# A hybrid decoder step: the inverse's transpose kept in the chunk recurrence, and every second paged sample gathered turned

## What is computed

```python
# the chunk recurrence, for each head and chunk
a_mat = where(strict, beta * (k @ k.T) * decay, 0) + eye(chunk)
w_v = solve(a_mat, v * beta)            # unit lower triangular
w_k = solve(a_mat, k * beta * exp(G))
# the paged decode, for each of 8 samples: 32 pages of 128 positions
past_c = cache_latent[page_table]       # 4096 x 256
past_r = cache_krope[page_table]        # 4096 x 64
past_k = cache_kscale[page_table]       # 4096 x 8
s = (q_lat @ c.T + q_rope @ kr.T) * ksc * SOFTMAX_SCALE
o_lat = softmax(s) @ c
```

## Time and profile before

| | |
|---|---|
| median of 3 runs | 3991.21 us |
| the profiled execution | 3988.52 us, of which the span is 3986.4 |
| TensorE, weight load, VectorE, ScalarE, GpSimd busy | 75%, 36%, 62%, 39%, 32% of the span |
| mean granted TensorE clock | 0.849 of 2.4 GHz |
| the chunk recurrence | 303.7 to 636 us |
| `mla_qkv` and the paged decode | 2205 to 2234 and 2234.6 to 2465.3 us |

### The profile page before, as it was taken

The page is one execution under the profiler, slowest core; times in us unless marked ns, Lnnn a source line. Parts: engine busy times, 40 slices in busy tenths (PEclk is TensorE's granted clock), DMA queues, the critical chain, the costliest instruction groups (busy, mean ns, idle before and its releaser), DMA issues. The chain is left out here.

```text
span 3986.4 us, 45941 instructions
## 1 busy us (share of the span) xinstructions
PE 3005.8 (75%) x14557; PEld 1439.4 (36%) x14557; DVE 2474.6 (62%) x6084; ACT 1535.0 (39%) x4402; POOL 1289.7 (32%) x1172
## 2 busy tenths in 40 slices
PE   7997888777666677768757798776777876666666
PEld 6886775322212122223313575322232222222221
DVE  2665443676676667767773343476677677667675
ACT  2352121444343344446432221344544444334332
POOL 0004330444434333333441110233334344334433
PEclk9998788988778788888878898888888988787778
DMA  2211002999999999999996453799999999999998
GB/s 89 73 51 55 13 13 71 404 420 416 420 414 418 405 397 387 411 366 384 402 421 244 165 204 144 291 375 390 381 375 415 405 404 421 413 420 413 411 421 334
DMA packets 234350, 1261.33 MB, mean 316 GB/s; under 512 B 32008, under 2 KB 71952, under 8 KB 97552
## 3 DMA queue, kind: packets, MB, share of 16 engines
q0 software_dynamic: 153600, 1133.58, 69.8%
q1 hardware_dynamic: 80528, 125.08, 9.1%
HBM read 1244.25 MB, written 14.19 MB: 316 GB/s over the span
## 5 line engine op out<-in xcount | busy, mean ns | idle before, releaser
L1951 PE MATMUL acc<-ring,diag 128*64 128x512 f32 x4096 | 1339.0, 751 | 751.3 <-ACT diag L1650 748.9
L1569 POOL DMA_INDIRECT ring<-in_uv,idx x1024 | 1119.1, 1093 | 1895.3 <-PE acc L1951 1635.2
L1761 DVE SCALAR_TENSOR_TENSOR ring<-ring,rep 128x1024 f32<-128x1024 f32 x1024 | 1230.6, 1221 | 368.9 <-DMA ring<-in_uv,idx 309.3
L1951 PEld LDWEIGHTS acc<-ring,diag 128*64 128x64 f32 x4096 | 250.3, 158 | 1494.2 <-ACT diag L1650 1317.8
L1642 ACT ACTIVATE hg<-hs 128x1 f32<-128x1 f32 x1024 | 203.7, 199 | 1141.1 <-DVE ring L1761 1139.1
L1650 ACT ACTIVATE diag<-const,hgg 128x64 f32<-128x64 f32 x1024 | 356.4, 348 | 33.4
L1646 ACT ACTIVATE hgg<-hg,weigh_by 128x1 f32<-128x1 f32 x1024 | 302.0, 295 | 33.2
L1883 PE MATMUL big<-xnT,w 128*128 128x264 f32 (+1 forms) x960 | 297.1, 435 | 0.0
L1883 PEld LDWEIGHTS big<-xnT,w 128*128 128x128 f32 x960 | 174.8, 203 | 185.0 <-issue 166.4
L298 PE MATMUL acc<-xnT,w 128*128 128x260 f32 x1024 | 230.2, 386 | 0.7 <-ACT inp L419 0.7
L298 PEld LDWEIGHTS acc<-xnT,w 128*128 128x128 f32 x1024 | 196.3, 192 | 38.4 <-issue 7.5
(11 more groups left out here) (571 smaller groups left out, 4057.7 us busy)
## 6 DMA issues: line engine op xcount, KB each, us to landing
w<-in_w_peer SPq DMA_DIRECT2D x64, 512.0 KB
w<-in_w_gdn SPq DMA_DIRECT2D x32, 512.0 KB, 3.6
ring<-in_uv,idx POOLq DMA_INDIRECT x1024, 12.3
wo<-in_w_mla_out SPq DMA_DIRECT2D x8, 1024.0 KB, 11.5
wo<-in_w_uq SPq DMA_DIRECT2D x8, 768.0 KB, 14.2
out_ssm_s<-states SPq DMA_DIRECT2D x4, 1024.0 KB, 5.1
wo<-in_w_gdn_out SPq DMA_DIRECT2D x4, 1024.0 KB, 8.2
sk<-in_keys SPq DMA_DIRECT2D x64, 64.0 KB
```

The lines of the kernel that those rows point to most:

```text
L1569: pool.indirect_dma_start(out=ring[:, c % RING, :], out_offset=None, in_=uv, in_offset=bass.IndirectOffsetOnAxis(ap=idx[u % 2][:, c:c + 1] ...
L1761: dve.scalar_tensor_tensor(ring[:, c % RING, 0:D], ring[:, c % RING, 0:D], 1.0, rep[:, 2 * a + c // RING, :], ALU.mult, ALU.mult, accum_ou ...
L1951: last = pe.matmul(acc[i][rows(j), :], diag[:, r, :], ring[:, r, D + HALF * j:D + HALF * j + HALF], start=r == 0, stop=r == RING - 1)
```

## The change

Three edits, made together.

In `gdn_seq`, `U` is turned only once per pair, before level 0, and all of it is copied to `T`. In levels 0 to 4 a second product of `U` and `X` follows each step on TensorE, and VectorE adds it into `T`, as it adds the step into `U`. VectorE's order at the head of a pair is changed: both heads' `U` first, then `Kb`, `kd`, `Vb` and `qk`.

In `mla_dec`, samples with `a` = 1 get their scores from a second copy of the cache, `cache_turned`, which is laid out in advance with 128 rows per page: a row is a latent (or rotary) channel and holds 320 numbers, 1280 bytes. It is fetched page by page, 32 indirect gathers of 128 rows (`pages_turned`), into one tile `turned`. These samples have no transposes and no copies of them; their latents are fetched as before for the value product, their rotary keys aren't. GpSimd's loop is written out, and in it the turned pages stand before the odd sample's factors and latents.

In `mla_qkv`, row numbers for these gathers are made from the page table: two more small loads on SP and three more VectorE operations on 256 columns.

```diff
@@ gdn_seq, ScalarE
-                    for j in range(LV):
-                        for a in range(2):
-                            after(act, at("flipped", i, 2 * j + a + 1))
-                            act.activation(half(T[a], j, 0), half(pC[a], j, 0), ACT.Copy).then_inc(s["flip_out"], 1)
+                    for a in range(2):
+                        after(act, at("flipped", i, a + 1))
+                        act.activation(T[a][:, :, :], pC[a][:, :, :], ACT.Copy).then_inc(s["flip_out"], 1)
+                    for j in range(LV):
@@ gdn_seq, TensorE
+                    for a in range(2):
+                        after(pe, at("seeded", i, 2 * a + 2))
+                        turn(pC[a], U[a]).then_inc(s["flipped"], 1)
                     for j in range(LV):
                         for a in range(2):
-                            after(pe, at("seeded", i, 2 * a + 2) if j == 0 else at("grown", i, 2 * (j - 1) + a + 1))
-                            turn(pC[a], U[a]).then_inc(s["flipped"], 1)
-                        for a in range(2):
-                            after(pe, at("flip_out", i, 2 * j + a + 1), at("lmask", i, 2 * j + a + 1))
+                            after(pe, at("paired_up", i, 2 * (j - 1) + a + 1) if j else at("flip_out", i, a + 1), at("lmask", i, 2 * j + a + 1))
...
-                            some(pB[a], X[j % 2][a], U[a], j, 1).then_inc(s["stepped"], 1)
+                            if j:
+                                after(pe, at("grown", i, 2 * (j - 1) + a + 1))
+                            last = some(pB[a], X[j % 2][a], U[a], j, 1)
+                            if j < LV - 1:
+                                last = some(pC[a], U[a], X[j % 2][a], j, 0)
+                            last.then_inc(s["stepped"], 1)
@@ gdn_seq, VectorE
                         for a in range(2):
                             after(dve, at("stepped", i, 2 * j + a + 1))
+                            if j < LV - 1:
+                                dve.tensor_tensor(half(T[a], j, 0), packed(pC[a]).rearrange("p (b s) -> p b s", s=2 << j), half(T[a], j, 0), ALU.add).then_inc(s["paired_up"], 1)
                             dve.tensor_tensor(half(U[a], j, 1), packed(pB[a]).rearrange("p (b s) -> p b s", s=2 << j), half(U[a], j, 1), ALU.add).then_inc(s["grown"], 1)
@@ mla_qkv, VectorE
+                dve.tensor_copy(pages.rowf[:, :], pages.all[:, :]).then_inc(s["gains"], 1)
...
+                dve.scalar_tensor_tensor(pages.rowf[:, :], pages.rowf[:, :], float(PAGE), pages.lane[:, 0:1].to_broadcast([P, NS * PAGES]), ALU.mult, ALU.add).then_inc(s["gains"], 1)
+                dve.wait_ge(s["gains"], 3)
+                dve.tensor_copy(pages.row[:, :], pages.rowf[:, :])
@@ mla_dec, GpSimd
+                def pages_turned(v):
+                    for g in range(PAGES):
+                        pool.indirect_dma_start(out=turned[:, g, :], out_offset=None, in_=core.i["cache_turned"],
+                                                in_offset=bass.IndirectOffsetOnAxis(ap=pages.row[:, PAGES * v + g:PAGES * v + g + 1], axis=0)).then_inc(s["lt1"], 16)
...
+                keys()
+                latents(0)
+                factors(0)
+                pages_turned(1)
+                latents(1)
+                factors(1)
+                for i in range(1, TURNS):
+                    after(pool, at("idx", i - 1, 1), at("flip", i - 1, NG))
+                    keys()
+                    after(pool, at("soft0", i - 1, 1))
+                    factors(0)
+                    after(pool, at("pv", i - 1, 1))
+                    latents(0)
+                    after(pool, at("idx", i - 1, 2), at("dotted", i - 1, 2 * NG))
+                    pages_turned(2 * i + 1)
+                    after(pool, at("soft1", i - 1, 1))
+                    factors(1)
+                    after(pool, at("pv", i - 1, 2))
+                    latents(1)
@@ mla_dec, TensorE
+                def latent(a, g, e, j):
+                    if a == 0:
+                        return cT[g % 2][:, e, j, :]
+                    first = PAGE * e + GRP * (BQ * g + j)
+                    return turned[:, :, first:first + GRP]
...
+                        if a and g == 1:
+                            after(pe, at("lt1", i, 16 * PAGES))
+                        after(pe, at("lined", i, n - 1))
                         if g == 1:
                             after(pe, at("staged", i, 2 * a + 2))
                         scores(a if g else 1 - a, (g - 1) % NG)
...
+                    if a:
+                        after(pe, (s["lc1"], i * 16 + 16), (s["ld1"], i * 16 + 16))
@@ mla_dec, VectorE
-                                apart(dve, at(f"lc{a}", i, 16), at(f"ld{a}", i, 16), at(f"lr{a}", i, 16), at(f"lk{a}", i, 16))
+                                apart(dve, at(f"lc{a}", i, 16), at(f"ld{a}", i, 16), at(f"lk{a}", i, 16))
+                                if a == 0:
+                                    apart(dve, at("lr0", i, 16))
                                 number(2 * i + 2 + a, a)
```

More of the change, by code:

```diff
@@ L510, in gdn_seq @@
     with Marks(core, "seq", rowed=4, summed=2, diff=4, decay=4, masks=4, made=2, signed=2,
[L511 removed]
+               crossed=2, turned=2, products=4, scaled=6, seeded=4, flipped=2, flip_out=2, paired_up=2 * (LV - 1), lmask=2 * LV, joined=2 * LV,
                joined_out=2 * LV, stepped=2 * LV, grown=2 * LV, wk=2, wk_out=2, u_made=2 * NT, u_out=2 * NT, s_made=2 * NT,
@@ L574, in _ @@
                             if j == 0:
-                                after(pool, at("products", i, 2 * a + 1))
+                                after(pool, at("products", i, a + 1))
                             if j >= 2:
@@ L762, in _ @@
                         dve.tensor_tensor(U[a][:, :, :], U[a][:, :, :], mask(C_ID), ALU.add).then_inc(s["seeded"], 1)
+                    for a in range(2):
+                        h = 2 * i + a
                         after(dve, at("turned", i, a + 1))
@@ L2152, in _ @@
                 sp.dma_start(pages.rest[:, :], core.i["rest"]).then_inc(s["page"], 16)
+                sp.dma_start(pages.lane[:, :], core.i["lane"]).then_inc(s["page"], 16)
+                sp.dma_start(pages.all[:, :], core.i["page_table"].rearrange("(o b) g -> o (b g)", o=1).to_broadcast([P, NS * PAGES])).then_inc(s["page"], 16)
                 sp.dma_start(pages.wukT[:, :, :], core.i["w_ukT"]).then_inc(s["wuk"], 16)
@@ L2252, in __init__ @@
         self.idx = [core.sbuf(ctx, "idx", [P, 1], U32) for _ in range(2)]
+        self.all = core.sbuf(ctx, "all", [P, NS * PAGES], mybir.dt.int32)
+        self.lane = core.sbuf(ctx, "lane", [P, 1])
+        self.rowf = core.sbuf(ctx, "rowf", [P, NS * PAGES])
+        self.row = core.sbuf(ctx, "row", [P, NS * PAGES], U32)
 def mla_dec(core, q, ckvT, krTs, ksc, wuv, os, pages):
@@ L2275, in mla_dec @@
         c = [core.sbuf(ctx, "c", [P, PER, KL]) for _ in range(2)]
-        kr = [core.sbuf(ctx, "kr", [P, PER, RD]) for _ in range(2)]
+        kr = core.sbuf(ctx, "kr", [P, PER, RD])
+        turned = core.sbuf(ctx, "turned", [P, PAGES, TURNED])
         ks = [core.sbuf(ctx, "ks", [P, PER, H]) for _ in range(2)]
@@ L2327, in latents, with keys @@
                         gather(a, c[a][:, PER // 2 * e:PER // 2 * e + PER // 2, :].rearrange("p j d -> p (j d)"), f"cache_latent{e}", name)
-                def keys(a):
-                    gather(a, flat(kr[a]), "cache_krope", "lr")
+                def keys():
+                    gather(0, flat(kr), "cache_krope", "lr")
+                def pages_turned(v):
+                    for g in range(PAGES):
+                        pool.indirect_dma_start(out=turned[:, g, :], out_offset=None, in_=core.i["cache_turned"],
+                                                in_offset=bass.IndirectOffsetOnAxis(ap=pages.row[:, PAGES * v + g:PAGES * v + g + 1], axis=0)).then_inc(s["lt1"], 16)
                 def factors(a):
                     gather(a, flat(ks[a]), "cache_kscale", "lk")
-                for a in range(2):
-                    keys(a)
-                    latents(a)
-                    factors(a)
-                with pool.Fori(1, TURNS) as i:
-                    for a in range(2):
-                        apart(pool, at("idx", i - 1, a + 1), at("flip", i - 1, NG * (a + 1)))
-                        keys(a)
-                        apart(pool, at(f"soft{a}", i - 1, 1))
-                        factors(a)
-                        apart(pool, at("pv", i - 1, a + 1))
-                        latents(a)
+                keys()
[17 more added lines that the diff above has]
+                    latents(1)
             @block.scalar
@@ L2475, in _ @@
                 turns(pe, turn)
-                after(pe, at("half0", TURNS, 0), at("half1", TURNS, 0), at("keyr", TURNS, 0), at("lined", TURNS, -1))
+                after(pe, at("lined", TURNS, -1))
                 scores(1, NG - 1)
@@ L2582, in turn @@
                         for g in range(NG):
```

(9 more changed lines are left out.)

65 lines of the change are left out of this document (39 added, 26 removed).

## The result

| | before | after |
|---|---|---|
| median, us | 3989.64 (4 runs: 3987.98 to 3994.84) | 4171.72 (4 runs: 4167.39 to 4175.7) |
| profiled execution, span | 3986.4 | 4165.6 |
| end of the recurrence (first weight load of the next stage) | 645.8 | 689.4 |
| first gather of the paged decode | 2234.6 | 2270.4 |
| the decode, to the next stage's weight load | 230.7 | 375.3 |

The changed kernel is slower: ratio 1.0454, 95% interval 1.0436 to 1.0472. That is 182 us, three times the 61 of the forecast and 89 us above the end of its range. The sign was right and both places were right; both sizes were wrong. The recurrence ends 43.6 us later than before (forecast 10.5), and the decode is 144.6 longer (49.5).

What follows compares the result with a forecast made beforehand. Recurrence and paged decode were both taken as bound by TensorE. Profiled 3988.5 + 10.5 (recurrence) + 49.5 (decode) + 1.2 (projections) = 4049.7; with 2.7 for the median, 4052 us, range 4020 to 4083.

Steps and rivals of the forecast that it cites:

- Part A, level: Recurrence: a level without other work becomes join, step and product, 5.25 us against 4.71, +0.54 us.
- Part A, the slow stretches: Recurrence: the level after the state read costs +1.0 us in three pairs; bound +18 for all Part A if slow stretches lengthen.
- Part A, the head: Head of a pair: first join done about 1 us sooner, slow step and product +1.5, net +0.3 to +0.5 us.
- Part B, the train: Decode: 32 indirect gathers per odd sample, 1.24 us apart, take 39.8 us, 159 in all.
- rival 3: Gathers run further apart, 1.39 us, adding 18.6 us: 4071 us; 14 in 100.
- Part B, the even half beside the train: Decode: TensorE finishes the even half during the gathers; odd half goes on after 44.8 us of a 66 us turn.
- Part B, the queue: Decode: odd sample's latents and factors stand behind the 32 gathers on GpSimd; late latents add 1.2 us to a turn.
- Part B, the row numbers: Projections before the decode: three more VectorE operations before a barrier, +1.2 us, bounds 0.6 and 1.6.
- Part B, the odd scores: Decode: without transposes odd steps take about 1.28 us instead of 2.26, saving 31 us of TensorE work over 4 samples.
- Rival 4: Odd scores read at half rate, 1.05 us more per step, +34 us: 4086 us; 4 in 100.
- Gathers hidden: Decode: GpSimd spaces gathers closer, so the odd half never waits, -25.5 us for the decode: 3977 us; 7 in 100.
- Levels shorter: Recurrence: second product slips beside the waits, each level loses its 1.18 us turn, -24 instead of +10.5: 4018 us; 12 in 100.

Runs made afterwards that it cites:

- a_order: Kernel before with only VectorE's new order at the head of a pair, all transposes kept: 3992.81 us, ratio 1.0006.
- d_train: Kernel before plus, once a turn, 32 GpSimd indirect gathers of 128 rows of 1024 bytes that nobody reads, ahead of the odd sample's latents: ratio 1.0402.
- b_direct: Decode part of the change alone, the turned pages fetched by plain DMAs from SP with the page number in a register: ratio 1.0075.
- d_busy: Kernel before plus 32 GpSimd memsets of 1024 columns once a turn, no added gathers: ratio 1.0161.
- the spaced train: Kernel before plus 16 unread gathers a turn, each followed by a GpSimd memset of about a microsecond: ratio 1.0144.
- d_groups: Kernel before plus 32 unread gathers a turn (rows of 896 bytes) in four groups of eight, two memsets of 1024 columns behind each group: ratio 1.033.
- d_eight: Kernel before plus a train of only 8 unread gathers a turn: ratio 0.9972.

## Why the prediction failed, point by point

**Part A, level.** Right. A level without other work is 5.36 us by the starts of its joins (forecast 5.25, before 4.71 in the earlier trace rows):

```profile
438.64 1.95 PE L626 MATMUL pA<-T,bI 128*128 128x64 f32 x16
...
444.00 1.95 PE L626 MATMUL pA<-T,gU 128*128 128x64 f32 x16
```

**Part A, the slow stretches.** Here terms were mis-sized: level 1 at the +0.54 of a level at full rate, and what follows the state read, where "as the fast rate comes back about then, I take +1.0". It did not come back. (By its own terms the sum for the four pairs is 4 x 3.0 - 0.5 = 11.5, not 10.5.) From the first join to the product with Kb pair 1 took 42.9 us before and 54.5 after. By the starts of the joins, level 0 took 2.5 us more, level 1 4.2, levels 2 and 3 0.65 each, level 4 with the read 0.8, level 5 2.8. So level 1 cost nearly eight times its +0.54, and level 5 cost 2.8 where the forecast had nothing. Level 5 has no second product; its join and the product behind it run at half clock throughout, where the earlier trace rows had the join at the edge of full clock:

```profile
457.13 3.62 PE L626 MATMUL pA<-T,bI 128*128 128x64 f32 x16
463.96 3.06 PE L620 MATMUL pA<-U,Kb 128*128 128x128 f32 x16
```

The forecast priced the added work at the rate that the rows before had at that place, 0.77 of full clock over the stretch. The change took the rate away too, to 0.69. The narrow products are not all of it: in a_order, with every transpose in place, level 1 took 2.7 us more and level 5 2.6 more, and the join of level 5 is as slow as after the change:

```profile
442.33 3.52 PE L626 MATMUL pA<-T,bI 128*128 128x64 f32 x16
```

There the level with the read took 2.7 us less, so that of the 11.6 us of this stretch 3.5 come with VectorE's order alone. In nine of the fifteen other traces with the old recurrence one pair loses the rate in the same way (45.5 us at 0.72). These levels stand at an edge, and what tips them is shown only so far: the order lowers the clock, the products lower it further, idle transposes raise it. The upper bound of +18 assumed "all the added work" at the slow rate, but not that work which was fast would become slow; measured +43.6 in the recurrence of the profiled execution, +46 us for the part alone.

**Part A, the head.** Right in kind: from nA to the first join it was 10.26 us before and is 8.41 after. The order by itself gave nothing over the whole: in a_order's trace the 1.9 us a pair that it saves ahead of the join are less than the 3.5 that the levels lose.

**Part B, the train.** Right: 32 gathers at 1.25 us (forecast 1.24), so rival 3, further apart, is refuted. By the estimate from the figures of the Trainium skill, "DMA: Bandwidth & Descriptors", section "Bandwidth", the transfers would have taken longer than the spacing; no run here shows that, since the spacing held at 1.25 us in rows of 64, 1024 and 1280 bytes alike, and the DMA engines moved 131 GB/s at less than half load.

**Part B, the even half beside the train.** This is the step that failed. The sum let TensorE do the rest of the even sample under the 38.5 us of the gathers, so that the odd half could start 41.3 us after the train began. It started 66.4 us after, at 2431.42:

```profile
2431.42 0.65 PE L2462 MATMUL pL<-turned,ql 128*32 128x128 f32 x16 [0.64 <-DVE lines L2590]
```

Of the 25.1 us, 0.4 are the gathers' own (38.9 us for 38.5), 4.6 lie between the time at which the last page should have landed and the restart at 2411.30, and 20.1 are the steps that were still to do. What follows took 23.5 us to the next train, against 24.7 in the forecast. So the turn is 89.9 where 66 was forecast, and it is no longer a wait for the pages that holds the odd half. That it is the train which stops the even half is shown from both sides: d_train puts the stop into the kernel before, and b_direct, with the same pages by plain DMAs, takes it out of the changed decode (+28 us instead of +146). No row of before shows the stop: in its whole trace the longest run at this spacing is eight gathers, 2234.6 to 2243.3. The forecast did say that "no gather of this size with so many behind it is in this trace", and yet gave this no price.

**Part B, the queue.** Right: the latents are issued late, 16 us behind the train and the factors' gather. d_busy measured what such an order costs by itself when GpSimd is held for 32 us a turn: 64 us.

**Part B, the row numbers.** Right: from the start of VectorE's last operation ahead of them to its first of the next stage it was 3.1 us before and is 3.9 after, +0.8 (forecast 1.2, bounds 0.6 and 1.6).

**Part B, the odd scores.** Right: the first steps are 1.27 to 1.62 us apart from 2431.42 on (forecast 1.28), their matmuls as long as an even sample's (0.65 us). Rival 4 is refuted. The 31 us of TensorE work are not all there: the decode's busy time fell only 7 us, at a clock of 0.70 against 0.91.

**The rivals on the other side.** Gathers hidden: no. Levels shorter: no, 5.36. What decided was among none of them: a train that stops the other engines, and a clock that the change lowered.

## What to carry to other kernels

Work that "lies beside" a queue must be seen running beside it: before it is costed at nothing, look for a stretch of the trace in which both ran at that density, and if there is none, put the sum without the overlap into the range. In a stretch at the edge of full clock, taking wide transposes out, or only changing the order at its head, can cost more in clock than in work; price both rates. Many short indirect gathers in a row from GpSimd are a bad way to bring pages; try plain DMAs with the page number in a register (here +28 us instead of +146, so not yet a gain), and give them a buffer that is free early enough.

## What the runs showed of the hardware that I had not expected

A dense train of indirect gathers stops the other engines. In a train of 16 or 32, 1.25 us apart, TensorE, VectorE and ScalarE fall silent or get out single instructions, in the turns behind the first from about the fifth gather until 3 to 8 us behind the last, whatever the size of the rows (64 to 1280 bytes). With gathers 2.08 us apart they work on until latents are missing, and so they do beside 32 memsets in a row.

How it works is open. The Trainium skill, "DMA: Bandwidth & Descriptors", section "Issuing engines are not separate DMA queues", says that DMAs run on the same 16 engines whichever engine starts them, and that starting them from several saves only time on the sequencer. Here the same rows cost 162 us from GpSimd and none that can be measured from SP. Part of the 162 is GpSimd's own time, which delays the gathers behind the train; by the turn less train of d_busy and d_train, an estimated 15 to 16 us a turn, some 60 in all, are not. One trace of it is in the records of instruction loads: of the 16 KB packets of queue q8, 5 came in the 44 us behind the second train of the changed kernel and none in its 39 us, and 4 came within 34 us of the spaced train; TensorE's instructions coming singly with "issue" ahead of them would fit a starved instruction queue. "Runtime: NRT & Kernel Launch", section "Instruction fetch mechanics", in the Trainium skill says that each sequencer loads its code in such blocks by a DMA queue of its own. But behind the third train of the changed kernel there are none either, and the kernel before shows none in its third and fourth turn, while TensorE works on; and VectorE's wait for scores long finished is not explained by it. Nor is it clear why eight alone stop nobody, when in d_groups the first eight of a train do, or why the sixteen at the start of d_eight's decode don't.
